# A hybrid decoder step on one core: value pages moved into the first sixteen gate units, two pairs in each

## The reference

```
kp = cache_k[layer, pages].reshape(n_ctx, FOX_HEADS, FOX_HD)
vp = cache_v[layer, pages].reshape(n_ctx, FOX_HEADS, FOX_HD)
...
pr = jax.nn.softmax(s, axis=-1).astype(va.dtype)
return jnp.einsum('hqk,khd->qhd', pr, va)
```

## Time and profile before

| | |
|---|---|
| median of 3 runs | 3101.51 us (3099.52 to 3107.52) |
| profiled execution, its own time | 3104.63 us |
| its span, first to last instruction | 3103.0 us |
| mean granted TensorE clock | 0.971 |
| TensorE matmuls busy | 2945.5 us, 95% of the span |
| VectorE, ScalarE, GpSimd busy | 62%, 40%, 6% |
| DMA traffic | 519.60 MB, mean 167 GB/s |
| gate units 1 to 31 in the trace | about 647 to 925 us |

### The profile page before, as it was taken

One profiled execution on the slowest core, in us unless ns is written; L12 is line 12 of the kernel. 1 busy time (PEld: TensorE's weight loads), 2 busy tenths in 40 slices (PEclk: granted clock), 3 DMA queues, 4 the chain that ended last, 5 costly groups with the idle time before them and its releaser, 6 DMA issues.

```text
span 3103.0 us, 60917 instructions
## 1 busy us (share of the span) xinstructions
PE 2945.5 (95%) x23119; PEld 2804.4 (90%) x23119; DVE 1918.7 (62%) x3707; ACT 1228.9 (40%) x2123; POOL 201.6 (6%) x227
## 2 busy tenths in 40 slices
PE   6999999989999998999998799999999978999999
PEld 6999868877878898999997799999999978999989
DVE  4467446545442345588868856656656687777764
ACT  4455421033330244445551144444444412444454
POOL 2100011000000000000004300000000042000000
PEclk8999979989899998999999999999999999999999
DMA  5545335547564444445542154454455512444543
GB/s 189 188 177 180 131 117 188 190 172 297 218 255 164 152 161 153 157 177 179 187 176 82 46 185 176 181 184 176 181 184 176 182 62 73 184 176 178 185 154 123
DMA packets 83934, 519.60 MB, mean 167 GB/s; under 512 B 11170, under 2 KB 11442, under 8 KB 30834
## 3 DMA queue, kind: packets, MB, share of 16 engines
q1 hardware_dynamic: 74882, 488.03, 43.4%
q0 software_dynamic: 7792, 25.95, 2.2%
q10 hardware_dynamic: 1152, 4.19, 0.4%
HBM read 508.75 MB, written 9.39 MB: 167 GB/s over the span
## 4 chain that ended last, share of the span: by engine, by line
PE 90%; DVE 6%; issue 2%; DMA 1%; ACT 0%; DVEq 0%; POOL 0%; POOLq 0%; SPq 0%; ACTq 0%
PE ps L577 25%; PE ps L578 25%; PE ps L579 24%; PE ps L1001 4%; PE ps L811 2%; DVE arena L1930 1%; DVE arena L2083 1%; DVE arena L1928 1%; PE ps L897 1%; PE ps L653 1%; PE ps L637 1%; PE ps L798 1%; PE ps L572 1%; DVE arena L1474 1%; PE ps L934 1%
## 5 line engine op out<-in xcount | busy, mean ns | idle before, releaser
L425 DVE TENSOR_TENSOR split<-arena,split 128x512 fp32r<-128x512 f32 x1568 | 1080.8, 692 | 840.2 <-ACT split L420 833.7
L420 ACT ACTIVATE split<-arena 128x512 fp32r<-128x512 f32 x1568 | 987.5, 631 | 1267.8 <-PE ps L579 1267.3
L577 PE MATMUL ps<-split 128*128 128x264 f32 x4224 | 1216.5, 288 | 45.2 <-DVE split L425 41.5
L578 PE MATMUL ps<-split 128*128 128x264 f32 x4224 | 1206.0, 286 | 0.0
L579 PE MATMUL ps<-split 128*128 128x264 f32 x4224 | 1205.1, 285 | 0.0
L577 PEld LDWEIGHTS ps<-split 128*128 128x128 f32 x4224 | 805.4, 191 | 71.1 <-DVE split L425 35.6
L578 PEld LDWEIGHTS ps<-split 128*128 128x128 f32 x4224 | 806.0, 191 | 0.5
L579 PEld LDWEIGHTS ps<-split 128*128 128x128 f32 x4224 | 801.5, 190 | 0.0
L577 PE MATMUL ps<-rounded,split 128*128 128x264 f32 x2048 | 584.1, 285 | 10.7 <-DVE rounded L2091 10.7
L578 PE MATMUL ps<-rounded,split 128*128 128x264 f32 x2048 | 584.4, 285 | 0.0
L579 PE MATMUL ps<-rounded,split 128*128 128x264 f32 x2048 | 580.6, 283 | 0.0
(11 more groups left out here) (323 smaller groups left out, 1702.3 us busy)
## 6 DMA issues: line engine op xcount, KB each, us to landing
arena<-in_wd SPq DMA_DIRECT2D x280, 1024.0 KB, 4.8
arena<-in_vd SPq DMA_DIRECT2D x128, 1024.0 KB, 4.8
arena<-in_kx SPq DMA_DIRECT2D x64, 512.0 KB, 4.6
arena<-in_vx SPq DMA_DIRECT2D x32, 512.0 KB, 6.7
arena<-in_vx POOLq DMA_DIRECT2D x32, 512.0 KB, 6.8
early<-in_state SPq DMA_DIRECT2D x8, 512.0 KB, 9.6
o_ss<-early ACTq DMA_DIRECT2D x8, 512.0 KB, 9.1
arena<-in_xT SPq DMA_DIRECT2D x1, 2112.0 KB, 8.6
```

The costliest lines, as they stand in the source:

```text
L420: nc.scalar.activation(ckh(q), at(WR + (s % 4) * D_MODEL + q * QW, QW), ACT.Copy).then_inc(hi_ready, 1)
L425: nc.vector.tensor_tensor(ckl(q), at(WR + (s % 4) * D_MODEL + q * QW, QW), as_f32(ckh(q)), ALU.subtract).then_inc(lo_ready, 1)
L577: mm(out, wh, xh, start=start, stop=False)
L578: mm(out, wh, xl, start=False, stop=False)
```

## The change

Value pairs 0 to 31 are computed in gate units 1 to 16, two in each, instead of one in each of units 1 to 31 (with two in the last). SP issues the even pages of two pairs in each of its rounds 1 to 15. VectorE's `value_rows` comes every second round, 2 to 16, and none is left behind the loop. The four buffers, the condition that lets pair p be loaded, and POOL's order stay as they are.

```diff
@@ SP
-                if u >= 2:
-                    load_values(sp, u, 0)
+                if 1 <= u < 16:
+                    load_values(sp, 2 * u, 0)
+                    load_values(sp, 2 * u + 1, 0)
@@ TensorE
-                if u >= 1:
-                    value_pair(u - 1)
-                if u == 31:
-                    value_pair(31)
+                if 1 <= u < 17:
+                    value_pair(2 * u - 2)
+                    value_pair(2 * u - 1)
@@ VectorE
-                if u >= 4 and u % 4 == 0:
-                    value_rows(u // 4 - 1)
-            value_rows(7)
+                if 2 <= u < 17 and u % 2 == 0:
+                    value_rows(u // 2 - 1)
```

## The result

The changed kernel takes 3133.34 us (median of 4 runs, 3127.86 to 3136.16) where the kernel before takes 3104.52 (4 runs): a ratio of 1.0088, 95% interval 1.0071 to 1.0104. It is slower by 29 us in the medians, 27 by the ratio: by more than the forecast and its range allowed. The profiled execution has a span of 3132.6 us, 29.6 more than before.

A forecast was written before the change was run, and what follows sets the result against it. It took the kernel as bound by TensorE's matmuls; -10.0 (end) + 11.2 (plain units) + 2.0 - 3.4 (states) + 3.4 (clock) = +3.2 us, about 3105 on the median, "the same"; range 3091 to 3121.

The forecast's parts named there:

- the 7.4 row: Profile row for two pairs going out together: odd page lands in 7.4 us, giving about 1.4 us wait a unit.
- The row of 8.4: Profile row for an odd page beside several 1 MB blocks: 8.4 us to land, giving 2.4 us wait a unit.
- The rival that used 8.4: Gate block slows POOL's second odd page: 2.4 us wait per plain unit, waits 22.6 + 2, 3126 us; chance 0.26.
- my 13.2: Waits in the two-pair units: 11.2 us in plain units plus 2.0 for states ahead of pages in SP's queue.
- The clock: Plain units: two of eight waits of 1.4 us would drop TensorE's clock, costing 3.4 us.
- The end: Last read-out to "up": 2.5 us for 11.9, 9.4 saved, plus 2.55 of clock, less 1.95 for pairs: 10.0 saved.
- The clock behind the end: Start of "up": full clock should hold, giving back half of 5.1 us, 2.55.
- Bandwidth: A changed unit moves 3.15 MB, needing 7.4 to 7.7 us at 408 to 423 GB/s; it lasts 7.95, so bandwidth suffices.
- Who pays: Units 2, 3 and 10 to 15 wait, 11.2 us; 4 and 16 nothing; 5 to 9 at most 0.4 in one.
- VectorE: `value_rows` every second round, 1.73 us, costs nothing; without cover, 1.73 in units 6 and 8, 3.5 in all.
- the queue rival: SP's gate block shares engines with POOL's second odd page; waits plus clock cost +24.8, 3126 us; chance 0.26.
- The low-rate rival: Mixed traffic at 339 GB/s: two-pair units grow by 1.35 us, states add 12, +15 in all, 3116 us; chance 0.08.

The follow-up runs named there:

- small_gates: The changed kernel with the loads of gate blocks 5 to 19 cut to 128 of 2048 columns; 3112.22 us.
- waits_only: The kernel before, with TensorE made to wait about 2.1 us before the value pair of units 9 to 14 and 25 to 30; 3135.08 us.
- small_all: The changed kernel with value pages 4 to 63 cut to 128 of 1024 columns and the transferred states to 64 of 1024; 3092.05 us.
- tail_sp2: The kernel before with two pairs in units 28 and 29, pair 31 in unit 30, and SP issuing all pages of pairs 28 to 31; 3100.56 us.
- odd_on_sp: The changed kernel with the odd value pages issued by SP as well, all four ahead of the gate block; 3112.63 us.
- no_states: The changed kernel with the states going out in unit 9 and in for unit 15 cut to 64 of 1024 columns; 3120.66 us.
- small_pages: The changed kernel with value pages 8 to 63 loaded to 128 of 1024 columns only; 3103.91 us.

## Why the prediction was wrong, point by point

**The step that failed** is the choice of the landing time. The prediction said: "The changed unit is nearest to the 7.4 row", and took 1.4 us of wait in a unit. The second odd page took 8.7 us in the median, not 7.4. The row of 8.4 was the right one: what they have in common is a block of 1 MB in SP's queue behind the page. I had set it aside because four blocks stood there and here is one; but this one block is worth 1.1 us of landing, for without it the page took 7.6 (small_gates), near the row that I chose. In that row the gate block went out 4 to 5 us behind the pages, here it goes out with them. The rival that used 8.4 gave 22.6 + 2 = 24.6 us of waits; 26.1 were measured, against my 13.2.

**The clock** was the second mis-sized term: 3.4 us forecast, 16.2 measured. I argued that waits of 1.4 us beside full-rate units would mostly not drop it. In the changed kernel most waits are of 2 to 3 us, and waits_only shows that at 2.05 us two in three are followed by a half clock at 1.56 us each. But I also priced the clock in plain units alone. Of my eight, units 2, 10 and 12 lost it in the split unit or the pairs, 6.1 us (unit 14 waited for 2.83 us and kept full clock); the other 10 us arose in units 5, 7 and 9 and beside the state matmuls of units 3 and 15, where I had put nothing. The part of units 3 and 15 is there without any wait as well (13.7 us in small_all, and 11.9 in tail_sp2 with the old placement, against 8.5 before), so how much of it is the change's and how much varies from one execution to the next stays open. The rival's 8 x 1.7 = 13.6 comes near to the total, but by luck: it isn't made up of eight losses in plain units.

**The end** was right in mechanism: 11.84 to 2.36 us is 9.5 saved (forecast 9.4), less 1.95. ("The other thirty pairs only change place ... nothing" and "units 17 to 31 are 0.97 shorter" weren't quite right: a unit without its pair is 1.17 shorter, a second pair in a unit adds 0.87, and this gave the 1.95 back.) The clock behind the end was overrated. I expected full clock in "up"; it still stood at 0.50 from 966.2 to 969.6:

```profile
966.20:969.60 3.40, 3.40 (x8) 2.60 (x9) 0.00 (x0) 0.00 (x0) 0.34 (x1) 0.50 0.74 209
969.60:973.00 3.40, 3.40 (x17) 2.86 (x16) 0.00 (x0) 0.00 (x0) 0.00 (x0) 1.00 0.97 417
```

That loses 1.7 us instead of 2.55, so the end by itself is worth 8.4 instead of 10.0.

**Bandwidth.** "So bandwidth just suffices, with nothing over" compared an average over full stretches with a need. Here loads can't start before buffers are free, and the changed stage has a lower DMA share (0.60) than the one before (0.63). Removing the order problem (odd_on_sp), the gate blocks (small_gates) or the states (no_states) gave 21, 21 and 13 us by the medians; all page and state traffic, 41. They overlap. Of the second odd page's 8.7 us the sharing with the gate block is 1.1; how much of the other 7.6 is sharing among the four pages, how much the slow start and end of a burst, stays open.

**Who pays.** Of units 2, 3 and 10 to 15 all but unit 11 waited, as said, and units 4 and 16 did not. But units 5, 7 and 9, to which I gave 0.4 us at most in one of them, waited for 2.1, 1.7 and 2.3 us as well. Units 6 and 8 between them didn't; I take it that a long unit lets the next one find its pages landed, but no run tests that.

**VectorE** cost nothing, as said. **The rivals:** the queue rival, at 3126, had the mechanism, the place and, with 24.8 of the 29.6 us of span, nearly the size. I gave it 0.26 and cut the range short of it. Of the 4.8 that remain 1.5 are waits, less 0.5 by which the waits of before were more than taken off, 2.6 clock in the stage, and 1.2 the end with what lies behind it (0.7 more where 2.55 less was forecast, against the 1.95 given back by packing). The low-rate rival (3116) had the right sign from the wrong cause: odd_on_sp moves the same bytes in 14.5 us less.

The sum with measured terms, in the profiled executions: +22.2 (waits) + 16.2 (clock) - 9.5 (end) = 28.9 for the stage, with pairs and packing even; 0.7 outside it.

## What to carry to other kernels

When work is packed closer, divide the time between freeing a buffer and needing it by the landing time as it will be with the new neighbours, not by bytes over bandwidth: here the distance fell from 13 to 7 us at the same number of buffers, and the loop "free, issue, land, use" became the clock of the stage. A short wait of the bound engine costs more than its length when the clock drops behind it; here it was half again. And take the gain of a reordering where it arises: moving the last few pairs one or two units forward, with the state loads spread, gave 14 us, where moving all of them lost 29.

## What the runs showed of the hardware that was not expected

A small load from GpSimd's queue can be as late as a large one, which alone took 5.1 us. In small_pages the 64 KB pages took this long, with full gate blocks beside them:

```profile
arena<-in_vx SPq DMA_DIRECT2D x28, 64.0 KB, 2.0
arena<-in_vx POOLq DMA_DIRECT2D x28, 64.0 KB, 4.9
```

The median of GpSimd's pages stands for two kinds. In small_all, where all of them are small, the first odd page of a round took 2.3 us in the median, and the second, out at the same time as SP's gate block, 5.0. It is the plainest sign of what the block does to a page in the other queue.

The filler kernel, which adds 208 matmuls at 650 to 830 us and nothing elsewhere, was slower by 57 us in code that it does not touch: in the first expert loop TensorE stood still twice, for 1.6 to 3 us each, in every round of about 102 us (seven rounds, 34 us in all), with half clock behind. In 1870 to 2000 us its DMA view has 13 packets on the instruction queue (first fence); the changed kernel has none there (second).

```profile
q8 instruction: 13, 0.21, 0.7%
```

```profile
q1 hardware_dynamic: 3248, 23.73, 50.1%
q14 instruction: 1, 0.01, 0.0%
```

Over the whole span the filler kernel has 130 packets on that queue and the changed kernel 65; 66 of them lie between 1850 and 2600 us, where the changed kernel has 3, and in each round some come together with the two stops. So it looks as if the loop's instructions were loaded again in each round there. Why in that kernel and not in the others was not tried; a difference between two kernels behind the edited stage should be looked for in that queue before it is put down to the edit.
